# Issuing the experts' down-projection loads from ScalarE's DMA queue instead of SyncE's

## What is computed

```
p_group = softmax(xt @ w_group + b_group)                 # 4 groups, top 1
e_val, e_idx = top_k(softmax(logits inside the group), 2) # 8 experts in a group, top 2
for gi in range(N_GROUPS):
    h = silu(einsum('md,edf->mef', xt, w_e1[gi])) * einsum('md,edf->mef', xt, w_e3[gi])
    out = out + einsum('mef,efd->md', h * combine[:, gi, :, None], w_e2[gi])
y = layer_norm(alpha * x1 + out)
```

## Time and profile before

| | us |
|---|---|
| median of 3 runs | 912.69 |
| lowest and highest | 907.22, 916.06 |
| the profiled execution's own time | 914.55 |
| its span in the trace | 912.8 |
| TensorE, mean granted clock | 0.942 |
| PE busy | 814.4 (89%) |
| weights and everything else through q1 | 161.30 MB |
| through q0 | 11.29 MB |

### The profile page before, as it was taken

How to read it: one execution, slowest core, us unless ns; L and a number is a source line. 1 busy time by engine, 2 the same in 40 slices (tenths; PEclk the granted TensorE clock), 3 DMA queues, 4 the chain that set the end, 5 groups by cost and what they waited for, 6 DMA issues and landing times.

```text
span 912.8 us, 11810 instructions
## 1 busy us (share of the span) xinstructions
PE 814.4 (89%) x4644; PEld 584.9 (64%) x4644; DVE 360.8 (40%) x628; ACT 241.1 (26%) x465; POOL 186.7 (20%) x172
## 2 busy tenths in 40 slices
PE   6999999998999999999999999936999998989900
PEld 6999984774567999999999844633343343433300
DVE  4899927895984101111011112452111111111168
ACT  4213232646677312222222100131111111111100
POOL 4000001000243343333433224212011111010000
PEclk9999999999898999999999999856999999999955
DMA  8333125031000822222222097462999999999472
GB/s 324 132 87 92 66 83 182 1 77 47 24 1 13 318 86 70 89 85 73 87 73 82 25 421 303 148 244 61 407 428 417 428 418 424 424 423 420 193 239 81
DMA packets 34354, 173.37 MB, mean 190 GB/s; under 512 B 7624, under 2 KB 8184, under 8 KB 25976
## 3 DMA queue, kind: packets, MB, share of 16 engines
q1 hardware_dynamic: 28232, 161.30, 46.4%
q0 software_dynamic: 6064, 11.29, 3.4%
HBM read 164.17 MB, written 18.87 MB: 201 GB/s over the span
## 4 chain that ended last, share of the span: by engine, by line
PE 79%; DMA 9%; DVE 8%; issue 2%; ACT 2%; SPq 0%; POOLq 0%; ACTq 0%; DVEq 0%
PE PS L662 38%; PE PS L963 12%; DMA expert<-in_w_e 7%; PE PS L851 7%; PE PS L983 5%; PE PS L645 5%; PE PS L772 2%; PE PS L720 2%; PE PS L918 1%; PE PS L872 1%; DVE x_tiles L1677 1%; PE PS L752 1%; PE PS L738 1%; DVE nb L1381 1%; PE PS L815 1%
## 5 line engine op out<-in xcount | busy, mean ns | idle before, releaser
L662 PE MATMUL PS<-x_hi,w_hi 128*128 128x288 f32 (+2 forms) x656 | 142.5, 299 | 9.0 <-DVE x_lo L1296 8.5
L963 PE MATMUL PS<-expert,moe_tmp 128*64 128x512 f32 (+1 forms) x512 | 136.8, 605 | 7.2 <-DMA expert<-in_w_e 5.8
L662 PE MATMUL PS<-x_lo,w_hi 128*128 128x288 f32 (+2 forms) x656 | 141.9, 298 | 0.0
L662 PE MATMUL PS<-x_hi,w_lo 128*128 128x288 f32 (+2 forms) x656 | 141.8, 298 | 0.0
L463 POOL TENSOR_TENSOR w_lo<-raw_ring,w_hi 128x1024 fp32r<-128x1024 f32 (+1 forms) x34 | 72.4, 2130 | 215.9 <-ACT w_hi L1046 215.9
L1046 ACT ACTIVATE w_hi<-raw_ring 128x1024 fp32r<-128x1024 f32 (+1 forms) x57 | 57.1, 1001 | 215.3 <-PE PS L662 211.0
L662 PEld LDWEIGHTS PS<-x_hi,w_hi 128*128 128x128 f32 x656 | 106.9, 192 | 9.1 <-POOL w_lo L463 8.4
L662 PEld LDWEIGHTS PS<-x_lo,w_hi 128*128 128x128 f32 x656 | 106.8, 191 | 0.0
L662 PEld LDWEIGHTS PS<-x_hi,w_lo 128*128 128x128 f32 x656 | 106.6, 191 | 0.0
L963 PEld LDWEIGHTS PS<-expert,moe_tmp 128*64 128x64 f32 (+1 forms) x512 | 49.5, 149 | 81.5 <-issue 79.6
L1313 DVE SCALAR_TENSOR_TENSOR conv_z<-attn_tmp,wdw,conv_z 128x576 f32<-128x576 f32 x120 | 90.6, 813 | 0.3
(11 more groups left out here) (272 smaller groups left out, 1077.5 us busy)
## 6 DMA issues: line engine op xcount, KB each, us to landing
expert<-in_w_e SPq DMA_DIRECT2D x32, 2048.0 KB, 26.7
expert<-in_w_e SPq DMA_DIRECT2D x32, 1024.0 KB, 28.6
raw_ring<-in_w_gate_t SPq DMA_DIRECT2D x24, 512.0 KB, 3.4
raw_ring<-in_w_glu_t SPq DMA_DIRECT2D x8, 512.0 KB, 4.7
raw_ring<-in_w_como_t SPq DMA_DIRECT2D x8, 512.0 KB, 3.6
heads<-in_w_out SPq DMA_DIRECT2D x1, 4096.0 KB, 14.1
x_rows<-x_tiles SPq DMA_DIRECT2D x8, 512.0 KB, 4.3
expert_out<-expert_rows SPq DMA_DIRECT2D x8, 512.0 KB, 7.0
```

Source lines behind the costliest of these rows:

```text
L662: mm = pe.matmul(half(name, s, 128, cols[s]), w[:, n % 2, at + 128 * k:at + 128 * k + 128], x[:, k, t0[s]:t0[s] + cols[s]], start=(k == 0 ...
L963: mm = pe.matmul(PS[r0:r0 + nr, 2, :].rearrange("p (s f) -> p s f", s=2), xgT[:, k, r0:r0 + nr], w13[s % NB][:, :, k, :], start=(k == 0), ...
```

## The change

SP's loop issues the up loads only; its second half, the wait for `e_y` with the down loads, goes. ACT issues the down loads instead, in its `result_step(u)`, directly after the eviction: for each expert of the stage, it reads the next expert's number from `order` into a register and issues the 1 MiB load. It waits once for `order_ready`, after its first `rows_step`. Buffers, semaphores, sizes and the expert that each buffer gets are the same, and the first six experts are still loaded by SP.

```
             sp.wait_ge(order_ready, 1)
-            expert_at = {}
-            for u in range(NS + 1):
-                if u < NS:
-
-                    for s in STAGES[u][1]:
-                        if s + NB < NE:
-                            r = STREAM[s + NB][1]
-                            expert_at[s + NB] = sp.value_load(order[0:1, r:r + 1], min_val=0, max_val=NE - 1)
-                            sp.wait_ge(e_h, u + 1)
-                            load_expert_up(expert_at[s + NB], s % NB)
-                if u >= 1:
-
-                    for s in STAGES[u - 1][1]:
-                        if s + NB < NE:
-                            sp.wait_ge(e_y, u)
-                            load_expert_down(expert_at[s + NB], s % NB)
+            for u in range(NS):
+                for s in STAGES[u][1]:
+                    if s + NB < NE:
+                        r = STREAM[s + NB][1]
+                        e = sp.value_load(order[0:1, r:r + 1], min_val=0, max_val=NE - 1)
+                        sp.wait_ge(e_h, u + 1)
+                        load_expert_up(e, s % NB)
...
                 evac_result(u % 2, 0).then_inc(e_ya, 1)
 
+                for s in STAGES[u][1]:
+                    if s + NB < NE:
+                        r, b = STREAM[s + NB][1], s % NB
+                        e = act.value_load(order[0:1, r:r + 1], min_val=0, max_val=NE - 1)
+                        act.dma_start(we[b][:, 4096:6144], a["w_e2"][bass.ds(e, 1)].rearrange("a p n -> p (a n)")).then_inc(we2[b], 16)
+
             act.wait_ge(tab_ready, 1)
             rows_step(0)
+            act.wait_ge(order_ready, 1)
             silu_step(0)
```

## The result

| | before | with the change |
|---|---|---|
| median, us | 914.38 (4 runs, 907.22 to 916.74) | 932.48 (4 runs, 929.17 to 934.32) |
| ratio | | 1.0207, 95% interval 1.0139 to 1.0276 |
| span of the profiled execution | 912.8 | 927.4 |

The change makes the kernel slower by 18.1 us (the interval is 12.7 to 25.2). The forecast was 928, or +15.5. The two profiled executions, from which the rows come, differ by less, 14.6 us, because the changed one (929.17) is the fastest of its four.

A forecast was written before the change was run, and what follows sets the result against it. The prediction took DMA engines and PE as almost balanced, with transfers setting the end. Its terms, 21.1 + 2 - 10.1 + 2.5, gave +15.5 us: 930 for the profiled execution, 928 for the median, range 909 to 937 (8 in 10).

The forecast's parts named there:

- What bounds the kernel: Expert part almost balanced between DMA engines (407 to 428 GB/s) and PE; the change moves only the order of transfers.
- Shares by packet: DMA engines alternate between queues by single packets, not bytes: 0.615 us an up packet, 0.31 down, 0.077 POOL's.
- Item 5, the lag: POOL's queue gets one turn in three, 17.7 us a stage against 11.8; PE waits 21.1 us for rows, then 2 more.
- Item 4: Down loads start 1.4 us later in their own queue; order among the weights stays about as it was: nothing.
- Items 6 and 7: PE's weight waits and slow result step go, 10.1 us; slower clock after PE's waits adds 2.5 us, between 0 and 5.
- Item 2: ACT issues 26 loads, 2.2 us a pair between its evictions, covered by 7.3 us: nothing.
- Item 3: ACT's wait for `order_ready`: the semaphore is up before ACT's first silu can start, so nothing.
- The signs: In the profile: three to five PE waits for rows, 4 to 6 us, from stage 7 or 8; gathers after 20 to 30.
- The order does not matter: Rival, chance 0.20: the same bytes across the DMA queues take the same time, 912, between 909 and 916.
- Shares by byte: Rival, chance 0.08: weight queues share by bytes, down loads overtake up loads before a hidden step; +6 us, 919.
- ACT is held: Rival, chance 0.06: ACT waits for queue room while issuing, 2 us in each of 16 stages; +30 us, 943.
- Faster: Rival, chance 0.08: up loads gain by the split and PE's waits for them go; 6.8 us at most, 906.

The follow-up runs named there:

- e6: The change with gathers of 16 rows instead of 128: 913.95, ratio 0.9998 to the kernel before; the kernel before with such gathers: 908.93, ratio 0.9962.
- e5: The change with every load of the loop cut into two by columns: 919.60, ratio 1.0071 to the kernel before.
- e8: The change with only the up loads cut into four, down loads whole: 929.14, ratio 1.0155 to the kernel before.
- e4: The change with ACT's down loads issued directly behind the wait for `e_y`, ahead of scatter wait and eviction: 931.80, ratio 1.0183 to the kernel before.
- e3: The change with every load of the loop cut into four by columns: 935.31, ratio 1.0228 to the kernel before.
- e9: The change with ACT's wait for `order_ready` moved ahead of its first `rows_step`: 931.70 in one run, beside the kernel before at 912.54.
- e2: The change with ACT issuing both up and down loads, SP none in the loop, so one weight queue: 915.82, ratio 1.0017 to the kernel before.
- e5's control: The kernel before with every load of the loop cut into two, all in SP's queue: 916.47, ratio 1.0026 to the kernel before.

## Why the prediction was right

**What bounds the kernel.** Right. A change that moves no work and only the order of transfers cost 2%, in an expert part that is balanced between DMA engines and PE. The expert part itself, from the first transposes to the last matmul, took 240.6 us before (625.15 to 865.72) and 257.1 now (623.12 to 880.19): +16.5; the rest of the profiled spans differs by -2, which is in the part ahead of the change.

**Shares by packet (the basis of items 4 and 5).** Right, and shown: by the counts 345 : 343 : 343 and the order of single packets, by e6, which takes packets out of q0, by e5, which makes turns shorter, and by e8, which upsets the bytes a turn gives. The Trainium skill's rule (DMA: Bandwidth & Descriptors, section Queues, rings and completion order) holds for the turns, but not for its packet of 9 to 17 descriptors: in these traces an engine goes on to the next queue after one row of a partition, 2 to 16 KiB by kernel.

**Item 5, the lag.** The pace was right: 17.7 us a stage forecast, 17.0, 16.6 and 14.8 measured; 17.7 turns of the 0.93 us measured make 16.5. The first late stage was 8 instead of 7, 4.4 us late instead of 3.4. The three stages after it added 13.1, which makes 17.5 us against the 21.1 of the forecast. The full lag ended when the forecast said, about 765, but not as it said: it was the up queue that ran dry, not the down queue (2 packets in 768 to 772, against 175 and 136), because PE, being late, released its buffers late: SP issued one up load at 750.1 and the next two at 768.7 and 769.8. The residue after that was put too low, at 2 us: from 792 on both weight queues had work again (69, 69 and 69 packets in 796 to 800), and stages 13 to 15 waited 5.8 us.

**Item 4.** Right that the order among the weights costs nothing: PE waits for none. Wrong on how late the down loads start. It had 1.4 us; in the eight stages where ACT waits for a scatter, ACT issues them 2.2 to 4.6 us after the end of the down-projection. e4 issues them without that wait and is still 16.7 us above before.

**Items 6 and 7.** The 10.1 us went completely. The slow steps after waits come to 6.1 us in the rows above (1.97 for 1.09, 5.69 for 3.65, and so on); in 721.3 to 725 the granted clock is 0.50, after the wait of 4.21 us, while after the one of 2.01 it is 1.00 in 738 to 740 and no step is slow. I had said that all but the last only run into the next wait, and that is what the spacing shows: the steps between 721.31 and 738.30 lose 2.9 us, and still the spacing is q0's. From stage 11's rows to the end the kernel needs 110.4 us, 7.6 more than the 102.8 that the earlier trace rows gives for the same stretch without its waits; residue and clock together were forecast as 4.5.

**Item 2.** Right: 0.34 us an issue, and PE does not wait for it. A pair adds 1.57 us between the two evictions instead of 2.2, since the first register load hides behind the first eviction. e3 shows where it ends.

**Item 3.** Wrong, by a small amount. I argued from the semaphore, which is indeed up in time. The wait's mere place moved the load of silu's table (1.28 us) behind a wait of 10.2 us, and PE lost 1.1 us. e9 shows it.

So the sum was 17.5 + 7.6 + 1.1 + 0.4 (the first hidden step, 10.00 us for 9.58) - 10.1 = 16.5 against 15.5: the largest term 3.6 too high, the residue with the clock 3.1 too low, one term missing. The mechanism and the pace were right on their merits; that the sum comes this close is partly luck, because two misses of over 3 us cancel.

**The signs.** Waits for rows from stage 8 on, none for weights, equal packet counts and short issues came as forecast. Not so the number and size of the waits, seven of 0.51 to 5.03 us, only two of them over 4, instead of three to five of 4 to 6; and the gathers landed after 34.0 us instead of 20 to 30.

**The rivals.** *The order does not matter* was given 0.20 and is refuted: e2 and the change move the same loads and differ in the number of weight queues, and the change is 17 us slower. Of what the Trainium skill says there (Trainium Kernel Development and Optimization, section Key Constraints) the shared engines hold, 423 GB/s in 700 to 800 in both kernels; that several issuers save only issue time does not, since here a second queue also took turns from a third. *Shares by byte* is refuted by the counts. *ACT is held* did not occur here but in e3 and e5. *Faster* did not come about, and its floor was misread: the engines were not full until 855.2 but 99% busy in 840 to 850 and 78% in 850 to 855.

**What stays open.** Why the loss is the same with three and with four buffers of rows was not settled. It may be bounded by how far weights can run ahead of PE, six experts; with either number the last up load lands at 848 to 849 us and is wanted 16 to 18 us later. No run varied the number of weight buffers, nor that of `ysb`. How many transfers ACT's queue holds before an issue is held was not measured either. None of the experiments on the real computation was faster than the kernel before: its transfers already come in the order of use, and its DMA engines are 99% busy up to 850 us.

## What to carry to other kernels

Before a transfer stream is moved to a queue of its own, count the packets of every queue on the DMA engines, not the bytes: a new queue with work takes one turn in every round, and the loser is the queue with many small packets, here a third one that the change did not touch. Where one queue already carries transfers in the order in which they are used, a second gave nothing in any of these runs. And look for the reserve of whatever is slowed: here it told when the damage began, and not how large it got.

## What the runs showed that I had not expected

- Cutting transfers makes an issuing engine wait. With loads in four parts an issue on ACT took up to 4.6 us, with halves up to 4.3; in the change, where they are whole, it took at most 0.45. SP is held too (up to 4.5 us in e5's control), but it has no evictions that PE waits for.
- The size of the rows changes the rate a little: in 700 to 800 the DMA engines moved 423 GB/s with rows of 16 and 8 KiB (the change), 416 with 8 and 4 KiB (e5) and 402 with 4 and 2 KiB (e3).
- A wait put between two activations can move the table load of the second behind that activation's own wait: 1.1 us, until e9 moved it back.
- POOL's scatters slowed with its gathers. In the change ACT and DVE waited 47.7 and 47.0 us for them, and PE never waited for those evictions.
